# Moving the low-rank products, the sigmoids and the decays of the next block forward in a chunked RWKV-7 and pooling layer on one core

## The reference, cut to what matters

```python
u = rms_norm(h, norm_gain) * (1 + scale) + shift
proj = u @ w_in                      # pool_v | pool_g | r | k | v | w_down | a_down | rg
y_pool = multiscale_pool(proj[pool_v]) * silu(proj[pool_g])
p = p + (token_shift(p) - p) * mu    # for r, k, v, w_down, a_down
w_log = -softplus(-(w0 + tanh(wd) @ w_lora_up)) - 0.5
decay = exp(-exp(w_log))
a = sigmoid(a0 + ad @ a_lora_up)
kk = normalised(k * k_k);  k = k * (1 + (a - 1) * k_a)
S_t = S_{t-1} diag(w_t) + (S_{t-1} a_t) b_t^T + v_t k_t^T;  y_t = S_t r_t   # a_t = -kk, b_t = kk * a
y_rwkv = (group_norm(y) + bonus) * silu(proj[rg])
h = h + gate * (concat(y_pool, y_rwkv) @ w_out);  out = rms_norm(h, final_gain)
```

## Time and profile before

| | us |
|---|---|
| median of 3 runs (2628.29 to 2630.16) | 2629.46 |
| the profiled execution's own time | 2628.31 |
| its span in the profile | 2626.6 |
| PE busy | 2547.5 (97%) |
| PEld busy | 2102.5 (80%) |
| DVE busy | 1520.5 (58%) |
| ACT busy | 1163.3 (44%) |
| POOL busy | 484.0 (18%) |

### The profile page before, as it was taken

One profiled execution on the slowest core, in us unless ns is written; L12 is line 12 of the kernel. 1 busy time (PEld: TensorE's weight loads), 2 busy tenths in 40 slices (PEclk: granted clock), 3 DMA queues, 4 the chain that ended last, 5 costly groups with the idle time before them and its releaser, 6 DMA issues.

```text
span 2626.6 us, 74898 instructions
## 1 busy us (share of the span) xinstructions
PE 2547.5 (97%) x30741; PEld 2102.5 (80%) x30741; DVE 1520.5 (58%) x3199; ACT 1163.3 (44%) x2626; POOL 484.0 (18%) x622
## 2 busy tenths in 40 slices
PE   6999999999999999999999999999999999999995
PEld 6777777777778888888888888888888888888883
DVE  2412121212157677777767777776677777667774
ACT  3324242323225455544445554454455445445542
POOL 3210101010121112211211121121112112111210
PEclk8999999999999999999999999999999999999997
DMA  8632322323210001000000101000010100001000
GB/s 338 255 112 81 110 93 99 102 90 112 81 65 10 26 29 39 26 34 26 26 26 26 42 26 34 26 26 26 26 42 26 34 26 26 26 26 42 26 18 25
DMA packets 68706, 153.08 MB, mean 58 GB/s; under 512 B 3977, under 2 KB 37342, under 8 KB 66398
## 3 DMA queue, kind: packets, MB, share of 16 engines
q1 hardware_dynamic: 63134, 130.08, 14.1%
q0 software_dynamic: 1680, 11.01, 1.0%
q10 hardware_dynamic: 3632, 7.87, 0.8%
HBM read 98.61 MB, written 50.33 MB: 57 GB/s over the span
## 4 chain that ended last, share of the span: by engine, by line
PE 74%; DVE 16%; ACT 4%; issue 3%; DMA 1%; DVEq 0%; SPq 0%; ACTq 0%
PE banks L949 20%; PE banks L355 16%; PE banks L984 9%; PE banks L387 8%; PE banks L932 7%; PE banks L1004 6%; DVE SM L1587 2%; DVE LA L1570 2%; DVE LA L1576 2%; PE banks L960 1%; PE banks L1112 1%; DVE t L1467 1%; DVE mix L1438 1%; DVE kk L1474 1%; DVE stmp L1519 1%
## 5 line engine op out<-in xcount | busy, mean ns | idle before, releaser
L949 PE MATMUL banks<-xT,w 128*128 128x128 f32 x5232 | 634.0, 279 | 0.0
L949 PEld LDWEIGHTS banks<-xT,w 128*128 128x128 f32 x5232 | 598.3, 192 | 31.1 <-issue 27.1
L1255 ACT ACTIVATE LX<-banks 128x512 f32<-128x512 f32 (+1 forms) x384 | 184.9, 524 | 642.6 <-DVE WT L1532 436.5
L355 PE MATMUL banks<-xT,w 128*128 128x256 f32 x2048 | 448.3, 381 | 4.8 <-ACT xT L475 4.8
L355 PEld LDWEIGHTS banks<-xT,w 128*128 128x128 f32 x2048 | 391.3, 191 | 65.3 <-issue 10.5
L932 PE MATMUL banks<-xT,w 128*64 128x128 f32 x6944 | 420.1, 274 | 0.0
L932 PEld LDWEIGHTS banks<-xT,w 128*64 128x64 f32 x6944 | 380.3, 137 | 6.3
L984 PE MATMUL banks<-wo,Y 128*128 128x512 f32 x512 | 234.3, 601 | 4.7 <-DVE Y L1492 4.7
L387 PE MATMUL banks<-wo,yc 128*128 128x512 f32 x512 | 224.8, 592 | 0.0
L672 DVE TENSOR_SCALAR gate<-gate 128x1024 f32<-128x1024 f32 x16 | 11.1, 694 | 367.7 <-ACT gate L495 367.7
L1532 DVE TENSOR_TENSOR WT<-banks,level_mask 128x256 f32<-128x256 f32 x256 | 102.6, 422 | 187.7 <-PE banks L1004 179.7
(11 more groups left out here) (185 smaller groups left out, 3587.6 us busy)
## 6 DMA issues: line engine op xcount, KB each, us to landing
x_in<-in_x SPq DMA_DIRECT2D x16, 1024.0 KB, 7.4
xr<-in_x SPq DMA_DIRECT2D x32, 512.0 KB, 4.3
xt_dram<-xT SPq DMA_DIRECT2D x32, 512.0 KB, 8.6
h_dram<-xr SPq DMA_DIRECT2D x32, 512.0 KB, 2.6
xT<-xt_dram SPq DMA_DIRECT2D x32, 512.0 KB, 3.3
gate_row<-h_dram SPq DMA_DIRECT2D x32, 512.0 KB, 4.3
out<-gate_row SPq DMA_DIRECT2D x32, 512.0 KB, 2.6
w<-in_w_in POOLq DMA_DIRECT2D x8, 1088.0 KB, 10.9
```

What stands on the lines that cost most here:

```text
L355: last = nc.tensor.matmul(bank[t // 2][:, (t % 2) * T1:(t % 2 + 1) * T1], w1[:, k, t * P:(t + 1) * P], xT[:, k, :], start=(k == 0), stop=( ...
L949: last = (by_halves if halves else nc.tensor.matmul)(bank[b][:, q * P:(q + 1) * P], w2[:, k, (t0 + q) * P:(t0 + q + 1) * P], xT[par][:, k, :],
L1255: s(nc.scalar.activation(to, of, ACT.Copy), lx_ready, hold=False)
```

## The change

The diff below is complete but for its context lines. TensorE: `low_rank` goes from behind `from_state(0)` to behind the slots of gap 2 and writes banks 4 and 7 (in the prologue still 2 and 3); the two `out_half` calls go from gaps 2 and 3 to gaps 3 and 4 and wait for `e_ready`, since they write the banks that ScalarE reads; one slot stands where `low_rank` stood. The number of slots stays 34, so the last `fill` of the block has five slots where it had six. ScalarE: both `exp_low_rank` calls go ahead of `take_step(3)`, the sigmoids ahead of and behind `take_step(4)`, and `decays` between `take_step(5)` and `residual_norm`. VectorE: the two `clamp` calls, `shift(n + 1, 1)` and `decay_sum` go between `factor(3)` and the residual. GpSimd: the subtraction for the decays goes ahead of the square of `kk`. `solve` itself is not touched by the diff.

```diff
-                def low_rank():
+                def low_rank(banks=(4, 7)):
...
-                            last = nc.tensor.matmul(bank[2 + i][:, p * P:(p + 1) * P], up[part, p * P:(p + 1) * P], rhs,
+                            last = nc.tensor.matmul(bank[banks[i]][:, p * P:(p + 1) * P], up[part, p * P:(p + 1) * P], rhs,
...
-                def out_half(h):
+                def out_half(h, ahead=False):
                     pv.wait(y2_ready, 1)
+                    if ahead:
+                        nx.wait(e_ready, NP * (h + 1))
...
-                def inverses(fill, other):
+                def inverses(fill, low_rank, other):
...
                         fill(3 if i < LV else 2)
-                        if i in (2, 3):
-                            other(i - 2)
+                        if i == 2:
+                            low_rank()
+                        if i in (3, 4):
+                            other(i - 3)
...
-                    inverses(fill, (lambda h: None) if first else out_half)
+                    inverses(fill, low_rank if ahead else lambda: None, (lambda h: None) if first else lambda h: out_half(h, ahead))
                     from_state(0, first)
-                    if ahead:
-                        low_rank()
+                    fill(1, halves=True)
                     solve(0)
...
-                    low_rank()
+                    low_rank(banks=(2, 3))
                     key_norm()
...
-                def exp_low_rank(i):
+                def exp_low_rank(i, banks=(4, 7)):
...
-                        hd(nc.scalar.activation(sig[:, i, p], bank[2 + i][:, p * P:(p + 1) * P], ACT.Exp, scale=-1.0,
+                        hd(nc.scalar.activation(sig[:, i, p], bank[banks[i]][:, p * P:(p + 1) * P], ACT.Exp, scale=-1.0,
...
                     take_step(2)
                     if ahead:
                         take_group(n + 1, 1)
+                        exp_low_rank(0)
+                        exp_low_rank(1)
                     take_step(3)
...
+                    if ahead:
+                        sigmoid(0)
                     take_step(4)
+                    if ahead:
+                        sigmoid(1)
                     take_step(5)
+                    if ahead:
+                        decays()
                     if not first:
                         residual_norm(n - 1)
                     if ahead:
                         take_group(n + 1, 2)
-                    if ahead:
-                        exp_low_rank(0)
                     take_u(0)
-                    if ahead:
-                        exp_low_rank(1)
...
                     if ahead:
-                        sigmoid(0)
                         key_scale()
-                        sigmoid(1)
                     take_u(1)
                     if ahead:
-                        decays()
                         take_group(n + 1, 3)
...
-                exp_low_rank(0)
-                exp_low_rank(1)
+                exp_low_rank(0, (2, 3))
+                exp_low_rank(1, (2, 3))
...
                 def head(n):
                     hd.block(n)
+                    hd.wait(G_ready, 1)
+                    hd(nc.gpsimd.tensor_tensor(egx[:, :, :], G[:, :, :], sig[:, 0], ALU.subtract), gprev_ready)
                     hd.wait(kk_ready, 1)
                     hd(nc.gpsimd.tensor_tensor(rn[:, :, :], kk[:, :, :], kk[:, :, :], ALU.mult), kk2_ready)
-                    hd.wait(G_ready, 1)
-                    hd(nc.gpsimd.tensor_tensor(egx[:, :, :], G[:, :, :], sig[:, 0], ALU.subtract), gprev_ready)
...
                     factor(3)
+                    if ahead:
+                        clamp(0)
+                        clamp(1)
+                        shift(n + 1, 1)
+                        decay_sum()
                     if not first:
                         residual(n - 1, 0)
-                    if ahead:
-                        shift(n + 1, 1)
                     last_factor()
...
                         shift(n + 1, 2)
                         key()
-                        clamp(0)
                     state_sum(0)
                     new_state(0, s, s_ready)
-                    if ahead:
-                        clamp(1)
                     take_r(1)
                     if ahead:
-                        decay_sum()
                         new_key()
```

## The result

The changed kernel takes 2680.49 us (2679.85 to 2680.51, 4 runs) beside 2629.14 us of the kernel before: a ratio of 1.0195, 95% interval 1.0177 to 1.0212. That is 51.35 us more; 2677 was forecast.

The account below looks back on a forecast made before the run. TensorE's queue, busy 97% of the span, was taken as the bound. Per block +1.09 + 1.06 - 0.54 = +1.61 us, 30 blocks +48.3, block 0 +0.5: 2677 us, own range 2665 to 2688, 8 in 10 2660 to 2691.

Parts of the forecast that it names:

- The low-rank products in gap 2: TensorE ahead of step 3: nothing idle takes them in, step 5 starts 1.09 us later; bounds 0.55 to 1.3.
- The decays ahead of `take_u(0)`: ScalarE's queue behind `take_step(5)`: `u_ready` comes 1.06 us later, TensorE idles about 1.4 us instead of 0.28.
- X: Start of step 5's weight loads; `u_ready` was forecast to reach TensorE at X + 6.88 instead of X + 5.82.
- the second loss: VectorE's `key` delayed to L + 1.4, still before the first `y_ps` at L + 1.71, so no extra cost.
- The tail: VectorE from `take_r(1)` to `state_sum(1)`: shortening gains 0.54 us per block, bounds 0 to 0.99; L1112 wait grows to 0.8.
- L: Start of a block's first L1058, forecast at X + 6.88; `state_sum(1)` was forecast to move from L + 10.23 to L + 9.69.
- the ring: Block as three pieces: TensorE from step 0 to L1058, on to `y_ps(1)`, then VectorE from `y_ps(1)` to step 0.
- Block 0: First block, no `residual_norm` in ScalarE's queue, so its copy is in time: about +0.5 us.
- Block 31: Last block, neither slots nor low-rank work: which gaps the two `out_half` cover is worth 1 us either way.
- TensorE's clock: Rival: clock falls in the new wait before L1058, another 1.1 us per block, 2711 us; chance 0.04.
- The faster: Rival: copy in time and VectorE not the bound, three waits lost, about 1 us per block, 2598; chance 0.05.
- the neutral rival: Only the copy before L1058 is in time: +0.25 us per block, 2637 us; chance 0.06.

Follow-up runs that it names:

- the two kernels with increments: Changed kernel with square first in the prologue, decays behind `take_u(0)`, one slot moved to the last fill, plus 32 or 96 idle semaphore increments before the loop: 2638.23, 2635.33 us.
- the pair with the decays behind: Changed kernel with decays moved behind `take_u(0)`, 2634.75 us; the same plus GpSimd's old square-first order in the prologue, 2628.59 us.
- the version with the slot: Changed kernel with square first in the prologue, decays behind `take_u(0)` and one slot moved from gap 2 to the last fill: 2608.89 us, ratio 0.9924.

## Why the prediction was right, point by point

**The low-rank products in gap 2: right.** +1.09 us was forecast; step 0 to step 5 went from 25.55 to 26.65. Doubling them added 0.87 more. One sign was named wrongly: step 3 starts not 1.09 us later behind step 2 but 2.34 us earlier (5.00 us instead of 7.34), since `out_half(0)` has left gap 2; it and `out_half(1)` come back behind steps 3 and 4, so that the sum up to step 5 is right. No wait appeared before steps 3, 4 and 5 of the blocks behind block 0, and the `out_half` calls do not wait for `e_ready`: the idle time of 0.76 us before steps 4 and 5 is the one that the block of before has behind each `out_half`.

**The decays ahead of `take_u(0)`: right in place and size.** Forecast X + 6.88, measured X + 6.94 and, in the other block of the turn, X + 6.85 (1702.38 to 1709.23). TensorE could have come at X + 5.33 (1622.26 to 1627.59 with the decays behind), where I had 5.5. Moving the three exponentials back brings 1.53 us per block, moving one 0.62. `key` ended at 1651.75, 0.42 us before the first `y_ps` let VectorE go on, so the second loss that I had excluded by 0.3 us did not come.

**The tail: right in kind, 0.15 us short.** `state_sum(1)` came at L + 9.67 (L + 9.69 forecast) and the wait before L1116 grew from 0.45 to 0.71 us (0.8 forecast). VectorE's work behind it was not unchanged, as I had it: from `state_sum(1)` to L1116 are 8.05 us, not 8.19; the multiplication of `kk` in it takes 0.69 us where it took 0.84 (below). Together 1.51 us in one kind of block (58.93 against 57.42) and 1.35 in the other (59.14 against 57.79), 1.42 on average instead of 1.61: 42.5 us instead of 48.3.

**GpSimd's swap: a term that the sum did not have.** I followed `head` only inside the ring, where it costs nothing, and did not ask who else calls it. Its cost in the prologue, 8.4 us by the run that puts it back and 6.2 by the pair with the decays behind (2634.75 and 2628.59), is larger than the error of any other term. It and the too large block term nearly cancel: that 2677 is so close to 2680.5 is luck.

**Block 0: +2.4 instead of +0.5.** The +0.5 counted on the copy being in time, and that held. But the cover that I counted on for the clamps, scan and sigmoids in gaps 3 and 4 is largely the `out_half` calls, and block 0 has none. The forecast named what this costs if the cover is gone (up to 1 us each; the three waits there are 1.50, 0.27 and 0.58 us) and did not see that in block 0 it is.

**Block 31** gained 1.1 us, a little more than the 1 us that I left for it.

**The rivals.** TensorE's clock did not fall: with an idle time of 1.58 us before them, the 16 loads of the first L1062 take 0.58 us as before, and the page's clock row is the same. Yet the rival was a near one: in the two kernels with increments the clock did fall inside the loop, behind five waits of 2.0 to 2.5 us. The faster and the neutral rival needed the copy in time; it was not. With the copy in time the kernel takes 2634.75 us, where the neutral rival had 2637; it counts no price for the prologue and 0.25 us more per block, and the run has the first and 0.11 us less per block (57.48 against 57.59). The claim that the slot taken from the end is not given back is shown from both sides: added ahead of `y_ps(1)`, work counts in full; a slot put back at the end wins the waits there, 0.91 us in the blocks without a jump, and no more.

## What to carry to other kernels

Before an operation is moved forward to shorten one engine's tail, read what it now stands in front of on its own engine, and when the bottleneck engine needs that: here 2 us of exponentials, harmless behind a copy, cost 1.5 us per block ahead of it. Filler work is worth something only in the stretch where the bottleneck engine would wait; moving it from there to a stretch without waits costs its length, here 0.91 us. Compare block with block before taking an average: the average of 0.58 us mixed this gain with a wait that had another cause. And follow each edited helper to all its callers, the prologue and the first and last turn above all: they lack the work that covers it elsewhere.

## What the runs showed of the hardware that was not expected

**The position of the loop's code.** 32 increments ahead of the loop made the kernel 29 us slower (2608.89 to 2638.23), 96 made it 26 us slower, and 32 instructions fewer, with two slots moved in block 0, made it 6 us faster. Most of this lies in blocks 1 to 30, 23.5 us more in each of the first two and 9.9 us less in the third: waits of TensorE behind the loop's jump that no semaphore explains and, with increments, the lower clock behind some of them. The differences of 1 to 2% that this study is about are as large as that, so only those tell an order of work apart whose traces have no such wait: the kernel before, the changed one, and those with the prologue or the decays put back. The other kernels can be compared by their blocks without a jump. The gain of the version with the slot in the whole time is a gain for this code position: the two shifted versions have the same order of work and are 0.2 and 0.4% slower than the kernel before.

**VectorE's instructions beside GpSimd's.** VectorE's busy time fell from 1520.5 to 1476.4 us with the same 3199 instructions. Three groups make up the difference, 45.6 us less together. Two of them are the clamps and the first part of `new_key`, groups of the whole execution. Kernel before:

```profile
L1456 DVE TENSOR_SCALAR sig<-sig 128x512 f32<-128x512 f32 x64 | 50.9, 796 | 15.1 <-ACT sig L1208 7.7
L1467 DVE TENSOR_SCALAR t<-sig,vec,oka 128x128 f32<-128x128 f32 x128 | 51.2, 458 | 21.1 <-ACT sig L1215 21.1
```

Changed kernel:

```profile
L1471 DVE TENSOR_SCALAR t<-sig,vec,oka 128x128 f32<-128x128 f32 x128 | 35.7, 343 | 1.2
L1460 DVE TENSOR_SCALAR sig<-sig 128x512 f32<-128x512 f32 x64 | 26.0, 407 | 11.3 <-ACT sig L1211 7.7
```

In the block of the earlier trace rows the first clamp took 1.27 us (1619.41 to 1620.68) with GpSimd's square of `kk` beside it (1619.36 to 1620.40), the second 0.43 us with GpSimd idle. The third group is the multiplication (27.5 and 22.3 us in the whole execution): `kk * rn` (two inputs in SBUF, 128x512) takes 0.849 us on average before and 0.693 in the run with the decays behind. Groups of instructions, 1000 to 2500 us of the kernel before:

```profile
L1474 DVE TENSOR_TENSOR kk<-kk,rn 128x512 f32<-128x512 f32 x26 | 22.1, 849 | 0.9
```

In the timeline of before GpSimd's second `BK` product still runs for 0.3 us when it starts (ends at 1631.62, start 1631.33), and the `new_key` of before starts 0.7 us ahead of the end of GpSimd's subtraction (1626.10 and 1626.83); in the changed kernel that product ends 1.5 us ahead (ends at 1660.69, start 1662.23). The overlap fits all three differences, but no run takes it apart from the rest.
